# Weight units of an fp32 transformer kernel: a third place for a rounded unit, and one exponential moved inside the narrow FFN

## Time and profile before

| what | value |
|---|---|
| three runs, us | 4445.46, 4451.7, 4448.62 (median 4448.62) |
| the profiled execution: time, span | 4442.89, 4441.1 us |
| TensorE (PE) busy | 4226.4 us, 95% of the span, 24311 matmuls |
| weight loads (PEld) | 3762.5 us, 85% |
| VectorE (DVE), ScalarE (ACT), GpSimd (POOL) busy | 72%, 41%, 32% |
| chain that ended last | PE 77%, DVE 13%, DMA 3%, ACT 3%, POOL 2% |
| mean granted TensorE clock | 0.976 of full speed |

### The profile page before, as it was taken

One profiled execution on the slowest core, in us unless ns is written; L12 is line 12 of the kernel. 1 busy time (PEld: TensorE's weight loads), 2 busy tenths in 40 slices (PEclk: granted clock), 3 DMA queues, 4 the chain that ended last, 5 costly groups with the idle time before them and its releaser, 6 DMA issues.

```text
span 4441.1 us, 61649 instructions
## 1 busy us (share of the span) xinstructions
PE 4226.4 (95%) x24311; PEld 3762.5 (85%) x24311; DVE 3208.3 (72%) x5013; ACT 1824.7 (41%) x3002; POOL 1422.5 (32%) x701
## 2 busy tenths in 40 slices
PE   7999989999999899989999899899999899999999
PEld 5887678887888798767999899799998699999887
DVE  5775558877887584464689998598886767785776
ACT  3233342323233544164333687233334544444444
POOL 0000300000000100000368787677772038665443
PEclk9999999999999998999999999899999999999999
DMA  6543215545545263201477799899994156678884
GB/s 268 226 160 131 76 58 202 216 167 193 234 193 191 92 245 143 95 20 67 145 229 241 257 334 334 289 371 359 357 350 174 48 183 214 215 242 282 291 287 164
DMA packets 286687, 926.48 MB, mean 209 GB/s; under 512 B 19136, under 2 KB 170816, under 8 KB 212288
## 3 DMA queue, kind: packets, MB, share of 16 engines
q1 hardware_dynamic: 249536, 788.30, 49.9%
q0 software_dynamic: 36864, 134.23, 8.6%
HBM read 837.52 MB, written 84.93 MB: 208 GB/s over the span
## 4 chain that ended last, share of the span: by engine, by line
PE 77%; DVE 13%; DMA 3%; ACT 3%; POOL 2%; issue 1%; SPq 0%; DVEq 0%; ACTq 0%; POOLq 0%
PE bank L1055 22%; PE bank L1057 22%; PE bank L1056 22%; DVE work L2454 3%; PE bank L1456 2%; PE bank L1041 2%; DVE work L2561 2%; PE bank L1224 1%; PE bank L1045 1%; DMA work<-in_up_rows,work 1%; POOL weight_ring_low L2709 1%; DVE weight_ring_low L2079 1%; DVE work L2563 1%; PE bank L1231 1%; PE bank L1256 1%
## 5 line engine op out<-in xcount | busy, mean ns | idle before, releaser
L2709 POOL TENSOR_TENSOR weight_ring_low<-weight_ring,up_high 128x1024 fp32r<-128x1024 f32 x240 | 650.0, 2717 | 1105.1 <-ACT up_high L1838 1103.1
L1057 PE MATMUL bank<-peer_h_high,weight_ring_low 128*128 128x256 f32 (+2 forms) x2240 | 702.9, 314 | 0.0
L1055 PE MATMUL bank<-peer_h_high,up_high 128*128 128x384 f32 (+1 forms) x2048 | 648.4, 317 | 33.3 <-POOL weight_ring_low L2709 31.4
L1056 PE MATMUL bank<-h_low,up_high 128*128 128x384 f32 (+1 forms) x2048 | 638.6, 312 | 0.0
L1055 PE MATMUL bank<-h_high,in_high 128*128 128x512 f32 (+1 forms) x1280 | 464.7, 363 | 5.8 <-DVE weight_ring_low L2079 5.5
L1925 ACT ACTIVATE down_high<-weight_ring 128x1024 fp32r<-128x1024 f32 x256 | 257.1, 1052 | 517.3 <-PE bank L1057 517.3
L1056 PE MATMUL bank<-h_low,in_high 128*128 128x512 f32 (+1 forms) x1280 | 464.0, 362 | 0.0
L1057 PE MATMUL bank<-h_high,weight_ring_low 128*128 128x512 f32 (+1 forms) x1280 | 464.0, 362 | 0.0
L2676 POOL TENSOR_SCALAR h<-work,params 128x256 f32<-128x256 f32 x12 | 11.8, 1000 | 1400.0 <-PE bank L1363 890.5
L1057 PEld LDWEIGHTS bank<-peer_h_high,weight_ring_low 128*128 128x128 f32 x2240 | 430.2, 192 | 3.8
L1055 PEld LDWEIGHTS bank<-peer_h_high,up_high 128*128 128x128 f32 x2048 | 394.0, 192 | 37.8 <-POOL weight_ring_low L2709 35.5
(11 more groups left out here) (374 smaller groups left out, 10299.0 us busy)
## 6 DMA issues: line engine op xcount, KB each, us to landing
weight_ring<-in_up SPq DMA_DIRECT2D x128, 1024.0 KB
weight_ring<-in_down SPq DMA_DIRECT2D x128, 1024.0 KB
weight_ring<-in_mod_w SPq DMA_DIRECT2D x112, 1024.0 KB
weight_ring<-in_ffn_in SPq DMA_DIRECT2D x88, 1024.0 KB
weight_ring<-in_ffn_out SPq DMA_DIRECT2D x64, 704.0 KB
gates<-work SPq DMA_DIRECT2D x40, 1024.0 KB, 8.7
gelu<-work SPq DMA_DIRECT2D x64, 384.0 KB
work<-gates SPq DMA_DIRECT2D x16, 1536.0 KB
```

Source lines behind the costliest of these rows:

```text
L1055: mm(dst, w_high, a_high, start=first, stop=False)
L1056: mm(dst, w_high, a_low, start=False, stop=False)
L1057: return mm(dst, w_low, a_high, start=False, stop=last)
L2709: G.tensor_tensor(ring_low[:, slot, w], ring[:, slot, w], up_high[:, n % 3, :].bitcast(F32), ALU.subtract)\
```

## The change

- A third place for a rounded weight unit, `third_high`, one for each kind of stage, in a part of the scratch memory that is unused at that time. Unit 2 of a stage is rounded into it (`unit_high`), all others go to k % 2 as before. TensorE and VectorE read it through the same helper.
- Unit 2 is rounded and split at the end of the norm, behind the last chunk of h, on ScalarE and on VectorE.
- Unit 3 takes the turn that unit 2 had (behind panels 0 and 1), unit 4 that of unit 3 (behind panels 2 and 3). Unit 4 has place 0, free since unit 0, and waits for unit 1 alone. From unit 5 on the turns are the old ones, and the turn behind panels 4 and 5 stays empty (`unit_behind`). In `mix` the order is changed by hand in the same way.
- In the FFNs `load_roots`, and with it in `ffn2_1` the exponential of the lambdas, moves behind `round_out(3)`; in `ffn2_1` the biases, gains and lambda sums on VectorE move behind `split_out(2)`.

```diff
+def unit_behind(p):
+    return p // 2 + 2 if p <= 4 else p // 2 + 1 if p >= 8 else None
...
+        third_high = dict(
+            ffn=high_low("third_ffn", [P, UNIT], work_at, (FC - 4) * T), mix=high_low("third_mix", [P, UNIT], work_at, shared_at + 2 * HEADS * T),
+            even=high_low("third_even", [P, UNIT], work_at, shared_at + 8 * T), odd=high_low("third_odd", [P, UNIT], work_at, odd_high_at + KC * T),
+            pee=high_low("third_peer", [P, UNIT], work_at, gelu_at))
...
+        def unit_high(name, k):
+            if k == 2:
+                return third_high["even" if name == "even" else name[:3]][:, :]
+            return high_of(name)[1][:, k % 2, :]
...
@@ round_unit
-                elif k >= 2:
-                    act.wait_ge(panel_done, plan.loads[weight_unit(name, s, k - 2)][4])
-                A(high_of(name)[1][:, k % 2, :], ring[:, u % SLOTS, :], ACT.Copy).then_inc(in_rounded, 1)
+                elif k > 2:
+                    act.wait_ge(panel_done, plan.loads[weight_unit(name, s, k - 2 if k != 4 else 1)][4])
+                A(unit_high(name, k), ring[:, u % SLOTS, :], ACT.Copy).then_inc(in_rounded, 1)
@@ norm_stage on ScalarE, behind the loop over the chunks
+                    round_unit(*s["next"], 2)
@@ norm_stage on VectorE, behind the last split_chunk
+                    split_unit(*s["next"], 2)
@@ ffn_stage on ScalarE
-                    if f + 2 < FC:
-                        round_unit(name, s, f + 2)
+                    k = unit_behind(2 * f + 2)
+                    if k is not None and k < FC:
+                        round_unit(name, s, k)
...
-                if name == "ffn2_1":
-                    act.wait_ge(lam_sums, 1)
-                    A(lam_tmp[:, 2:4], lam_tmp[:, 0:2], ACT.Exp).then_inc(lam_exps, 1)
-                load_roots(name)
                 for v in range(2, 2 * KC):
                     round_out(v)
+                    if v == 3:
+                        if name == "ffn2_1":
+                            act.wait_ge(lam_sums, 1)
+                            A(lam_tmp[:, 2:4], lam_tmp[:, 0:2], ACT.Exp).then_inc(lam_exps, 1)
+                        load_roots(name)
@@ mix_stage on ScalarE
-                round_unit(name, s, 2)
                 round_unit(name, s, 3)
+                round_unit(name, s, 4)
...
-                for k in range(4, 6):
-                    round_unit(name, s, k)
+                round_unit(name, s, 5)
@@ ffn_stage on VectorE
-                if name == "ffn2_1":
-                    add_biases(len(plan.mod_read), trunk, MODS)
-                    second_gains()
                 for dc in range(KC):
                     if dc + 1 < KC:
                         split_out(2 * dc + 2)
+                    if name == "ffn2_1" and dc == 0:
+                        add_biases(len(plan.mod_read), trunk, MODS)
+                        second_gains()
@@ mix_stage on VectorE: split 3, 4, 5 where 2, 3 and 4 and 5 stood
-                        split_unit(name, s, 2)
+                        split_unit(name, s, 3)
...
-                split_unit(name, s, 3)
+                split_unit(name, s, 4)
...
-                    if c % 2:
-                        split_unit(name, s, 4 + c // 2)
+                    if c == CC - 1:
+                        split_unit(name, s, 5)
```

More of the change, by code:

```diff
@@ L1818, in mixer_stage @@
             def mixer_stage(name, s):
-                for k in range(2, 12 if name == "even" else 6):
+                for k in range(3, 12 if name == "even" else 6):
                     round_unit(name, s, k)
@@ L1862, in copy_gates @@
                           ACT.Copy).then_inc(gates_copied, 1)
-                for k in range(2, 8):
+                for k in range(3, 8):
                     round_unit(name, s, k)
@@ L2154, in ffn_stage @@
                         .then_inc(pair_free, 1)
-                    if f + 2 < FC:
-                        split_unit(name, s, f + 2)
+                    k = unit_behind(2 * f + 2)
+                    if k is not None and k < FC:
+                        split_unit(name, s, k)
                     mod_sums(name, f)
@@ L2393, in rotated_chunks, with copied_panels @@
                     p += 1
-                    if p % 2 == 0 and p // 2 + 1 <= last:
-                        split_unit(name, s, p // 2 + 1)
+                    if p % 2 == 0 and unit_behind(p) is not None and unit_behind(p) <= last:
+                        split_unit(name, s, unit_behind(p))
                 return p
-            def copied_panels(name, p, dsts, s=None, split=None, shift=0):
+            def copied_panels(name, p, dsts, s=None, shift=0):
                 for k, dst in enumerate(dsts):
@@ L2407, in copied_panels @@
                     p += 1
-                    if split is not None and k % 2 and k // 2 < len(dsts) // 2:
-                        split_unit(name, s, split + k // 2)
+                    if s is not None and p % 2 == 0 and unit_behind(p) is not None:
+                        split_unit(name, s, unit_behind(p))
                 return p
@@ L2417, in even_stage @@
                     if c % 2:
-                        split_unit(name, s, 2 + c // 2)
-                p = copied_panels(name, 4, [na_k[:, c, :] for c in range(4)], s, 4)
+                        split_unit(name, s, unit_behind(c + 1))
+                p = copied_panels(name, 4, [na_k[:, c, :] for c in range(4)], s)
                 p = rotated_chunks(name, s, p, df_q, 4, True)
@@ L2441, in peer_stage @@
                 nt = t // P
-                copied_panels(name, 0, [pq[:, 0:nt, c, :] for c in range(HP - 4)], s, 2)
+                copied_panels(name, 0, [pq[:, 0:nt, c, :] for c in range(HP - 4)], s)
                 copied_panels(name, HP - 4, [pq[:, 0:nt, c, :] for c in range(HP - 4, HP)])
```

13 lines of the change are left out of this document (7 added, 6 removed).

## The result

The changed kernel takes **4411.32 us** (median of 4 runs, 4410.08 to 4415.91), the kernel before 4449.32 us on the same chip (4 runs, 4445.46 to 4451.7). The ratio is 0.9919, with a 95% interval of 0.9907 to 0.9931. Another measurement of the same pair gave 4412.74 (5 runs) against 4447.64 (21 runs), ratio 0.992 [0.9907, 0.9934], so 35 to 38 us. The base of the forecast held: it started from 4448.62, and the kernel before took 4446.94 to 4449.32 us wherever it was measured again.

The account below looks back on a forecast made before the run. TensorE was taken as the bound, so only its idle or lower-clock time could be won; 6.5 + 1.1 + 5.6 + 4.3 + 7.2 = 24.7 us off 4448.62 gave 4423.9, stated as 4424.0 us, range 4418 to 4429.

Parts of the forecast that it names:

- What bounds the kernel: TensorE is busy 95% of the span; its waits for the third unit's rounding and split can be won.
- What the gap of a wide stage costs: At the third unit of six wide stages: 0.86 us idle plus 0.23 us, 1.09 us each, 6.5 us together.
- `ffn2_1`: The narrow FFN: 2.8 us from its third-unit gap, 7.2 us from its output half, including 2.73 us of lower clock.
- the returned table loads: Before split 4 in `ffn2_1`'s output half: 1.29 us from load to user, covered by 0.4 us, so no cost.
- `odd`: At its third unit: 2.55 us from the gap, 0.4 us wait remaining, plus 1.76 us of lower clock; 4.3 us.
- `peer_1`: At its third unit: the same 2.57 us gap as `ffn2_1`, plus 0.23 us, so 2.8 us.
- the sum: Over all stages: 6.5 + 1.1 + 5.6 + 4.3 + 7.2 = 24.7 us, earlier starts carrying through.
- rival A: In `odd` and `ffn2_1`'s output half the clock gives nothing back: 4.5 us fall away, 4428.5 us; chance 0.12.
- B: Earlier starts are absorbed in `peer_0`; only `odd` and `peer_1`, 7.1 us, remain: 4441.5 us; chance 0.06.
- C: In the four narrow stages the wait moves to unit 3, costing 11.6 us: 4435.5 us; chance 0.06.
- D: A late load of unit 2 holds ScalarE in the norms; at 4 us a stage slower, 4464 us; chance 0.02.
- The range: For the whole kernel 4418 to 4429 us, from 3 us of run spread either side and 2 us for misjudged margins.

Follow-up runs that it names:

- e11: The changed kernel with the third place taken away in `ffn1_1` alone; 4414.65 us, ratio 0.9927 to the kernel before.
- e12: The kernel before with the narrow FFN's output-half moves and the third place in `ffn1_1` alone; 4432.94 us, ratio 0.9965.
- e3: The changed kernel without the output-half moves, so the third place and unit 2 in the norm only; 4420.6 us, ratio 0.994 to the kernel before.
- e4: The kernel before with the output-half moves alone, no third place; 4441.32 us, ratio 0.9986.
- e5: The kernel before with eight idle matmuls added before the sixth unit of `ffn1_0`; 4450.98 us, ratio 1.0009.
- e8: The kernel before with the output-half moves and the third place in `peer_0` alone; 4435.82 us, ratio 0.9968.
- e2: The changed kernel, unedited, for a second profile; 4412.74 us, ratio 0.992 to the kernel before.
- e6: The changed kernel with eight idle matmuls added before the sixth unit of `ffn1_0`; 4418.28 us, ratio 0.9931 to the kernel before.
- e7: The changed kernel with the third place taken away in `peer_0` alone; 4413.86 us, ratio 0.9924 to the kernel before.
- e15: The changed kernel with the third place taken away in `peer_0` alone, ended behind `peer_0`; 3390.57 us.

## Why the prediction was right, and where it failed

**What bounds the kernel, right.** All ten stages' waits for the third split were time on the path; taking them out shortened every one of the ten stages.

**What the gap of a wide stage costs, right.** 1.09 us each was forecast. `ffn2_0`, where the clock doesn't move, gives 1.08 on the mean of nine profiles against nine, so the step from 0.86 us of idle time to 1.09 of lost time was needed. Single pairs scatter about it: 0.9 in `ffn1_0`, 0.8 in `even` from before to after, and 1.2 to 1.4 in `ffn1_1` told apart by e11 and e12.

**`ffn2_1`, right.** 2.8 + 7.2 = 10.0 forecast, 10.05 measured from profile to profile; e3 and e4 split it 3.5 and 7.0. Taken at nothing and in fact so: the rounding behind the last chunk, and the returned table loads. The loads, in the changed kernel:

```profile
1656.70 1.28 ACT L1705 ACT_TABLE_LOAD   x1
1658.00 0.21 ACT L1705 ACTIVATE small<-small 128x2 f32<-128x2 f32 x1
1658.22 1.28 ACT L1620 ACT_TABLE_LOAD   x1
1659.52 0.20 ACT L1620 ACTIVATE small<-eps 128x1 f32<-128x1 f32 x1
```

Each user starts 1.30 us behind the start of its load, and TensorE goes from one output chunk to the next after 0.34 us. The 2.66 us of the Trainium skill ("ScalarE: Activation LUTs", What ACT_TABLE_LOAD costs), weighed in the prediction, don't show here; the row of before was the better price.

**`odd`, right in the profile, and its second term a draw.** 3.7 us came where 4.3 were forecast. The gap's share was 2.25 (150.55 in e3 against 152.80 in e4, e5 and e8, which all have the gap and not the fall) against 2.55, and the remaining wait, 0.51 us behind the rotation, is the one that was worked out. The clock's share was 1.5 against 1.76, and it is there only in the executions that have the fall: three profiles of six with the gap. "A gap of 0.4 follows dense work, so I take the clock to stay up" held in all six with the gap closed; what was wrong is that the fall was taken as a fixed cost of the gap. That the profile from which it was read has the fall is luck.

**`peer_1`, 2.5 to 5.0** (e2, after) where 2.8 was forecast: two profiles with 6.39 and 3.08 us of clock cost.

**The step that failed is the sum: "Every later stage starts from semaphores of the one before, so an earlier start carries through."** It credits each stage with its own closed gap, lets each keep the rest of its length, and counts the clock in two places only, behind `odd`'s gap and behind that of `ffn2_1`'s output half. Three stages did otherwise, and their terms of 1.09 us were too small. (1) `mix_0` gave 2.5: the 3.4 us at the lower clock that the kernel before has 187 us behind the norm, far from any gap that was priced, fall away, about 1.5 us. (2) `ffn1_1` gave 2.8: 1.4 of them are clock behind its norm and come from what has changed ahead of it, not from its own gap (shown by e11 and e12). Together these are most of the 4.2 us by which the timed gain up to `even`, 20.8, exceeds its terms, 16.6. That the clock might give back more than was counted, in stages whose gaps cost none of it, was in no case; rival A doubted even what was counted. Why these two stretches go with the change stays open. (3) `peer_0` gave 6.4 us as timed, roughly, and why stays open. Together that is 9.5 us of the 10 to 13 that were missed; the rest, 1 to 4 us, is in `odd` and `peer_1`, where 35 to 38 less 27.2 leaves 8 to 11 us against 7.1. For `peer_1` one cause is seen and was not priced: with its gap open, a fall of the clock in three profiles of six.

**The rivals.** A (the clock gives nothing): refuted, `ffn2_1`'s output half gave its 7 us, and `mix_0` and `ffn1_1` gave more. B (absorbed in `peer_0`): refuted in the other direction, 20.8 us saved before `peer_0` had become 27.2 behind it. C (the wait moves to unit 3) and D (ScalarE held by a late load): neither shows at any of the ten stages' heads in the changed kernel's profile: at and just behind the third unit's place the only idle time is `odd`'s 0.51 us, and no rounding of a unit 2 waited.

**The range** took the runs' 3 us of spread for the kernel's own. With 21 runs the kernel before spreads over 12 us, and the changed one over 5; since the median hardly moved, this did not cause the miss.

## What to carry to other kernels

A wait that repeats at the head of every stage is worth more than its idle time: add what the overlap of back-to-back matmuls loses, and expect 1.1 us for 0.86. Price a fall of the clock behind a gap of some 2.6 us as a chance and not as a fixed cost: here 9 of 21 with the gap and 0 of 21 without, 1.5 us each in `odd`. One profile doesn't tell which. When many such waits go, stretches at the lower clock come and go in stages that were not priced, and VectorE's products meet GpSimd's splits in another order; my estimate, from the 4.2 us up to `even` and the 5.3 that `peer_0` gave beyond its term, is to keep some 5 to 10 us for it on a kernel like this, even if every gap is priced right. Before a sum is trusted, time the kernel cut off behind a stage: up to `even` 5 runs agreed within 3 us, while the whole kernel spread over 12.

## What the runs showed that was not expected

- **The same gap is followed by the lower clock in some executions and not in others.** Three gaps of 2.57 to 2.79 us: 9 of 21 profiles with them open, 0 of 21 with them closed.
- **The clock behind a norm can repeat from one execution to the next, or not.** `ffn1_1` cost 2.1 to 2.2 us of it in nine of 18 profiles and 3.6 to 3.7 in the other nine, split by what the stages before it had, without an exception; `mix_1`, one stage on, took 143.7 or 145.3 us in profiles with identical work up to there.
- **A profile of an edited kernel needs a control.** e6's slower `mix_0` and `mix_1` look like the work of its eight idle matmuls, until e7 shows the same two without them.
- **VectorE's 128x1024 product takes 1.22 us alone and about 3 us beside GpSimd's 2.4 us split**, and where the two chains stand against each other went with TensorE's wait of one tile: 10.0 or 4.5 us, which the time of the kernel did not keep (e7, e15).
- **One stage holds nearly all of the scatter of the kernel before**: 13.6 us in `peer_0` between two executions, at most 1.0 in each other stage of the same two.
